# Gates laid out by feature, routing on the raw residual, and a finer last quad in each expert stage

## The reference, cut to what matters

```python
# first block, end
x = x + memory_cross_attention(...)              # o @ w_o
h = rmsnorm(x, ffn_norm)
g_logits = h @ wg_router + bg_router             # 4 groups
e_logits = h @ we_router + be_router             # 32 experts
# second block
gate_na, gate_mla = columns of (h @ w_in)        # 1024 wide each
merged = (sigmoid(gate_na)  * (y_na  @ w_proj_na)
          + sigmoid(gate_mla) * (y_mla @ w_proj_mla))
x = x + gate1 * (merged @ w_out)
h2 = rms_norm(x, g_norm2) * (1.0 + scale2) + shift2
# in both expert layers, for each expert e
a = silu(hg) * hu * gate[..., None];  out += a @ w_down[e]
shared = (silu(t @ w_sg) * (t @ w_su)) @ w_sd    # second block
```

## Time and profile before

| | us |
|---|---|
| median of 3 runs | 1127.06 (1125.6 to 1129.26) |
| profiled execution | 1125.87, span 1123.9 |
| PE busy | 988.9 (88%) |
| DVE busy | 461.2 (41%) |
| ACT busy | 206.0 (18%) |
| loads moved | 360.33 MB, mean 321 GB/s |
| mean granted clock of TensorE | 0.959 |

### The profile page before, as it was taken

How to read it: one execution, slowest core, us unless ns; L and a number is a source line. 1 busy time by engine, 2 the same in 40 slices (tenths; PEclk the granted TensorE clock), 3 DMA queues, 4 the chain that set the end, 5 groups by cost and what they waited for, 6 DMA issues and landing times.

```text
span 1123.9 us, 12966 instructions
## 1 busy us (share of the span) xinstructions
PE 988.9 (88%) x4504; PEld 477.8 (43%) x4504; DVE 461.2 (41%) x1089; ACT 206.0 (18%) x438; POOL 126.0 (11%) x167
## 2 busy tenths in 40 slices
PE   6999999887887677689999998998999998688777
PEld 4445543455332222144556544654544434233232
DVE  1796823345121111025754223677434335643234
ACT  2214301321111111021633403110211210000000
POOL 0000101000000000000000000005545543110000
PEclk9999999888998888899999999999999999889899
DMA  9744787978899999978984164079999997999997
GB/s 357 270 163 174 276 338 255 424 298 326 329 412 421 423 421 421 418 176 312 417 348 150 76 234 168 19 282 414 413 381 375 363 351 262 416 405 416 415 418 287
DMA packets 72272, 360.33 MB, mean 321 GB/s; under 512 B 19744, under 2 KB 21972, under 8 KB 45664
## 3 DMA queue, kind: packets, MB, share of 16 engines
q1 hardware_dynamic: 60816, 315.96, 70.9%
q0 software_dynamic: 11408, 43.74, 10.2%
HBM read 337.61 MB, written 30.31 MB: 327 GB/s over the span
## 4 chain that ended last, share of the span: by engine, by line
PE 71%; DMA 17%; DVE 5%; SPq 3%; ACT 2%; issue 2%; DVEq 0%; ACTq 0%
PE bank L998 31%; DMA wring<-in_w_pack 16%; PE bank L1265 9%; PE bank L1173 6%; PE bank L1123 5%; PE bank L1276 5%; PE bank L1206 4%; PE bank L1216 3%; PE bank L1009 2%; SPq L526 1%; PE bank L1363 1%; DMA wring<-in_w_ada 1%; PE bank L1063 1%; PE bank L1030 1%; PE bank L1037 1%
## 5 line engine op out<-in xcount | busy, mean ns | idle before, releaser
L998 PE MATMUL bank<-wring,hT 128*128 128x512 f32 (+3 forms) x608 | 248.5, 570 | 13.8 <-DVE hT L2637 8.5
L998 PEld LDWEIGHTS bank<-wring,hT 128*128 128x128 f32 x608 | 113.8, 200 | 139.4 <-issue 130.4
L1173 PE MATMUL bank<-wring,kT 128*32 128x512 f32 x944 | 119.8, 650 | 42.2 <-DMA wring<-in_w_pack 39.7
L1265 PE MATMUL bank<-wring,qT 128*128 128x512 f32 x256 | 114.6, 599 | 2.9 <-issue 2.9
L1173 PEld LDWEIGHTS bank<-wring,kT 128*32 128x32 f32 x944 | 30.9, 118 | 124.7 <-issue 71.6
L1216 PE MATMUL bank<-yT 128*128 128x512 f32 x128 | 65.1, 635 | 21.4 <-DVE yT L2508 5.7
L1206 PE MATMUL bank<-wring,yT 128*32 128x512 f32 x480 | 60.8, 626 | 23.2 <-DMA wring<-in_w_pack 14.3
L1265 PEld LDWEIGHTS bank<-wring,qT 128*128 128x128 f32 x256 | 48.3, 193 | 59.1 <-issue 59.1
L998 PE MATMUL bank<-wring,yT 128*128 128x512 f32 x160 | 70.5, 595 | 0.7 <-ACT yT L1622 0.7
L909 POOL DMA_INDIRECT PRT<-xn_parts_dram,part_now x64 | 65.6, 1025 | 28.4 <-issue 16.9
L1123 PEld LDWEIGHTS bank<-kT,x 128*128 128x128 f32 x512 | 62.8, 204 | 13.7 <-issue 11.6
(11 more groups left out here) (445 smaller groups left out, 1097.4 us busy)
## 6 DMA issues: line engine op xcount, KB each, us to landing
wring<-in_w_pack SPq DMA_DIRECT2D x132, 1024.0 KB, 15.3
wring<-in_w_pack SPq DMA_DIRECT2D x96, 512.0 KB, 14.8
wring<-in_w_pack SPq DMA_DIRECT2D x16, 2048.0 KB, 8.9
wring<-in_w_ada POOLq DMA_DIRECT2D x18, 1024.0 KB, 10.6
y_dram<-gateB SPq DMA_DIRECT2D x4, 4608.0 KB, 21.0
kT<-in_w_ada POOLq DMA_DIRECT2D x6, 1024.0 KB, 9.7
wring<-in_pack_z.0 SPq DMA_DIRECT2D x1, 2048.0 KB, 9.7
wring<-in_pack_z.2 SPq DMA_DIRECT2D x1, 2048.0 KB, 15.7
```

Source lines behind the costliest of these rows:

```text
L998: mm = nc.tensor.matmul(b[:, 0:n], lhs(k, t), w[:, k, c0:c0 + n], start=(k == 0), stop=(k == nk - 1))
L1173: mm = nc.tensor.matmul(bank[lane[j], 0, :], xqT[:, k, lane[j]], w[:, (k % 4) * 512:(k % 4 + 1) * 512], start=(k == 0), stop=(k == KD - 1))
L1265: mm = nc.tensor.matmul(bank[:, s, :], xT[:, s, k, :], item_gate_up(s)[:, k, :], start=(k == 0), stop=(k == KD - 1))
```

## The change

Five parts.

1. **Routing on the raw residual.** PE turns `x` itself as soon as `wo` is added; the gain goes in as before, and the factor per token is multiplied into the 36 logits on DVE, since it is one number per token. `tmp` is no longer written. The turns of t = 0 stand ahead of `wo.1.1`, and the logits of t = 0 between the two turns of t = 1.
2. **The list of experts later.** `quad_experts` and `experts_taken` move on DVE behind the hidden values of quad 1; on PE `experts_turned` moves behind its last down half, and the wait for the list to quad 2.
3. **Gates by feature.** `y.4` to `y.7`, `pna` and `pmla` are computed turned: the weights are held and 256 tokens stream. `merged0` and `merged1` are then the lower and the upper 512 features of all tokens, `wout2` reads them from `Z`, and `mgT` goes. The fixed experts' gate and up loads wait for the end of `wout2`, and the shared expert's weights are issued ahead of them.
4. **The last quad.** Down half 0 is loaded and computed in two pieces (its 256 hidden features in two halves of 128), four DMAs of 256 KB each, with one sum of half 1 between them and one behind.
5. **The shared down product sooner**, ahead of quad `duos + 3`.

`FIRST_BANK` moves by 4 in the second segment, as four bank uses go.

```diff
-    one += columns("wo", V)
-    for t in range(2):
-        one += [(f"xT3.{2 * t}", V), (f"xT3.{2 * t + 1}", V), (f"route1.{t}", V)]
+    one += [("wo.0.0", V), ("wo.1.0", V), ("wo.0.1", V), ("xT3.0", V), ("xT3.1", V), ("wo.1.1", V)]
+    one += [("xT3.2", V), ("route1.0", V), ("xT3.3", V), ("route1.1", V)]
...
+                if g == 1:
+                    piece(2, 0, 1024)
+                    piece(3, 1024, 1024)
+                else:
+                    piece(5, 1024, 1024)
+                    piece(4, 0, 512)
+                    piece(6, 512, 512)
...
-                sp.wait_ge(E("bank_filled"), group_at[f"mgT.{2 * s + 1}"][2])
+                sp.wait_ge(E("bank_filled"), group_at["wout2.1.1"][2])
                 load_item_gate_up(s, fixed_expert_of(s))
...
-                    if n == 1 and first:
-                        experts_turned(1)
+                    if second:
                         copied(pe, "items1")
...
                     else:
-                        down(0)
-                        combined(1)
-                    combined(0)
+                        down(0, (0,))
+                        pe.wait_ge(E(f"moe{n}_quad_half_copied"), i)
+                        combined_tile(0, 1)
+                        down(0, (1,))
+                        combined_tile(1, 1)
+                        combined(0)
...
+                    shared_down()
                     quad(duos + 3, False, ahead=3)
                     with pe.Fori(duos + 4, quads_n) as i:
                         quad(i, False)
-                    shared_down()
...
+            for n, t in ((0, 0), (1, 0), (0, 1)):
+                output_columns(n, t)
+                ada_steps(1)
+            residual_turned(0, 0)
+            residual_turned(0, 1)
+            output_columns(1, 1)
             pe.wait_ge(E("router_loaded"), 32)
+            residual_turned(1, 0)
+            b = opened("route1.0")
+            group_logits(b, 0, 0)
+            closed(group_logits(b, 0, 1))
+            residual_turned(1, 1)
+            b = opened("route1.1")
...
+            def turned_blocks(key, job, rows_, first_block, nk):
+                b = opened(key)
...
+                for j in range(2):
+                    c0 = P * (first_block + j)
+                    for k in range(nk):
+                        mm = nc.tensor.matmul(b[:, j * S:(j + 1) * S], w[:, k, c0:c0 + P], rows_[:, k, :], start=(k == 0), stop=(k == nk - 1))
...
+            pe.wait_ge(E("rows_ready"), ready_value("merged0"))
+            b = opened("wout2.0.0")
+            linear_steps(b, "wout2.0", merged_rows, 0, last=4)
+            b_next = opened("wout2.1.0", 1)
+            linear_steps(b_next, "wout2.1", merged_rows, 0, last=4)
+            pe.wait_ge(E("rows_ready"), ready_value("merged1"))
+            closed(linear_steps(b, "wout2.0", merged_rows, 0, first=4))
+            closed(linear_steps(b_next, "wout2.1", merged_rows, 0, first=4))
+            both_columns("wout2", ("wout2.0", "wout2.1"), merged_rows, 1, (0, 0))
...
                     hidden(1)
+                    quad_experts()
                     next_rows(1)
+                    experts_taken()
...
+                V.scalar_tensor_tensor(gl[:, t, :], b[:, 0:4], st[:, t:t + 1], rowv("router_group_b"), ALU.mult, ALU.add)
```

More of the change, by code:

```diff
@@ L194, in plan_groups @@
     for t in range(2):
-        two += [(f"mgT.{2 * t}", A), (f"mgT.{2 * t + 1}", A), (f"wout2.0.{t}", V), (f"wout2.1.{t}", V)]
+        two += [(f"wout2.0.{t}", V), (f"wout2.1.{t}", V)]
     for t in range(2):
@@ L1824, in y_columns, with gate_blocks @@
                 copy(f"y.{c}.{t}", Z[:, t, c0:c0 + w], func=func)
+            def gate_blocks(c, half):
+                c0 = (GN0, GM0)[c // 6] + 512 * half
+                copy(f"y.{c}.{half}", Z[:, c % 2, c0:c0 + 512], func=ACT.Sigmoid)
             for c in (0, 1, 3, 2):
```

151 lines of the change are left out of this document (92 added, 59 removed).

## The result

| | before | after |
|---|---|---|
| median, us | 1128.12 (1125.1 to 1134.29, 16 runs) | 1120.88 (1118.6 to 1127.11, 16 runs) |
| profiled execution, us | 1125.87 | 1119.93 |
| its span, us | 1123.9 | 1117.7 |
| ratio | | 0.9936, 95% interval 0.9922 to 0.9951 |

The change makes the kernel 0.64% faster, some 7 us. The sign was forecast, the size was not: 16.1 us and 1110.5 were, and 1120.88 lies above the forecast's range of 1107 to 1118. The profiled executions differ by 5.9 us.

A forecast was written before the change was run, and what follows sets the result against it. Full DMA stretches bound the kernel; their start and the work behind their last byte count. Terms 4.9 + 4.0 + 3.0 + 3.2 + 1.0 = 16.1 us off 1125.87 gave 1109.8, or 1110.9 from the median; forecast 1110.5, range 1107 to 1118.

The forecast's parts named there:

- parts 1 and 2, to quad 1's down: Routing and expert list ahead of the first stage: its full DMA stretch starts 8.9 us sooner, bounds 4.3 and 9.5.
- part 4, first stage's tail: Behind the first stage's last landing: split down half and earlier sums gain 3.0 us, after 0.3 for smaller loads.
- part 3, to the turn of the normed rows: Gates and wout2: sets of transposes and waits for copies go, gaining 3.2 us, bounds 2.7 and 3.8.
- part 5, and part 4 at the end: Second stage's end: moving the shared product gives 0, the split down half 1.0 us, bounds 0.3 and 1.3.
- the sentence on what is late next after part 2: Quad 2's down weights land at about 292.5, just when PE wants them; failure of this thin cover costs up to 2 us.
- part 2: List of experts ahead of quad 2's selection: selection starts 2.3 us sooner and keeps the upper clock; 4.0 us taken.
- the first stage keeps its start: Rival, chance 0.15: routing and list changes give 4 us instead of 8.9 at the first stage; time 1115.5.
- Its other ground: Same rival, first stage: the clock may fall earlier with so many small matmuls in a row; no separate size.
- low bounds of all terms together: Whole kernel: every term at its lowest gain gives 1117.6 us.
- part 1: First router: raw-residual routing brings the second logits forward, gaining 4.9 us; 2.0 if all at the lower clock.
- 0.3 us for the small pieces: First stage's last 2 MB: halving loads to 256 KB costs 0.3 us, bounds 0 and 1.
- weight loads: Case at the gates, chance 0.04: 256-column records, each with a weight load, take longer than half a 512-column one.

The follow-up runs named there:

- e10: Changed kernel with the last quad's old, unsplit down tail in the first expert stage alone; ratio 0.9928 to the kernel before.
- e1: Changed kernel with one 1 MB lane of the third quad's loads issued behind quad 2's down weights instead of ahead; ratio 0.9893 to the kernel before.
- e14: Changed kernel with 7 filler matmuls ahead of quad 2's down, where PE waits for its weights; ratio 0.9936 to the kernel before.
- e3: Changed kernel with 24 filler matmuls in PE's two gaps at the second router (16 and 8); ratio 0.9871 to the kernel before.
- e8: Kernel before with only the last quad's split down half, in both stages, shared product at its old place; ratio 0.9971 to the kernel before.
- e4: Kernel before with only the gates and projections by feature, with their wout2 and fixed loads; ratio 0.9987 to the kernel before.
- e6: Changed kernel with one lane behind quad 2's down weights, filler at the second router and the shared product at its old place; 1111.45 us, ratio 0.9842.
- e7: Kernel before with only the routing on the raw residual and the later list of experts; ratio 0.9936 to the kernel before.
- e2: Changed kernel with the shared product back at its old place, between the last quad but one and the last; ratio 0.9915 to the kernel before.
- e11: Changed kernel with 24 filler matmuls in the second stage's last quad, shared product at its new place; ratio 0.9938 to the kernel before.
- e9: Changed kernel with 24 filler matmuls ahead of quad 2's down; ratio 0.9956 to the kernel before.

## Why the prediction was half right

Step by step, in the profiled executions, gains in us:

| step | forecast | measured |
|---|---|---|
| parts 1 and 2, to quad 1's down | 8.9 | 9.4 |
| what of it reaches quad 2's second down | all | 4.1; 5.4 lost |
| part 4, first stage's tail | 3.0 | 2.9 from quad 2 to block 2, at most some 1 of it the new tail's (e10) |
| part 3, to the turn of the normed rows | 3.2 | 3.3 |
| second router | 0 | 4.1 lost |
| part 5, and part 4 at the end | 1.0 | 0 (3.5 and 3.4 us from the last packet to the add) |
| sum | 16.1 | 6.1 (6.14 at the adds) |

**The step that failed first** was the sentence on what is late next after part 2. It named the right weights, and it had them land at 292.5 with a failure worth "up to 2 us". They landed at 294.6, and 5.4 us were lost. The price was taken as the wait alone, and that too low: 2.4 of wait and 3.0 of lower clock behind it (e1, e14). The rival "the first stage keeps its start" is in the main this mechanism; its sum of 4 for parts 1 and 2 is what was measured, and it got 0.15. Its other ground, that many small matmuls in a row bring the clock down earlier, did not show: the clock fell at the end of the wait, between 294 and 296 us.

**The step that is missing** is the second router. The clock was weighed only at the places where the change removes a wait; I did not ask whether the stretches that the change does not touch keep theirs. The low bounds of all terms together gave 1117.6, and 1120.88 lies beyond it because no term held a loss of clock in an unchanged stretch. The row of the kernel before with 0.57 at 704 to 708 was there to see. e3 shows that the loss is the clock, e8 and e10 that it comes with part 4 of the first stage. So part 4 there gives 3.5 us to the kernel before and at most some 1 us beside parts 1 and 2, less 4.1 either way. Why a tail 210 us ahead decides it is not settled.

**Right in size:** part 1 (quad 1's selection 5.1 us sooner for 4.9), part 2 (4.3 us more up to quad 1's down for 4.0, the selection at 3.81 us, the upper level), part 3 (3.3 in the changed kernel and in e4, for 3.2), the tails on the kernel before (e8: 3.5 and 1.2), and 0.3 us for the small pieces. The gate records settle the case "weight loads", 0.04 in the forecast: that records of 256 columns, of which part 3 has 384 for 192 of 512, each with a weight load of its own, would take longer than half of one of 512. In the chain after, 32 of 256 columns take 6.91 us, 0.216 each, as in the earlier trace rows, so two take 0.432 where one of 512 took 0.429, and e4 shows a gain of 3.3. The eight loads of 256 KB at the end, issued by SyncE, cost an estimated 0.3 us together by e8 (386 GB/s for 411 over 2 MB).

```profile
547.78 6.91 PE bank L1563 x32
```

**Part 5** was priced at nothing because the last byte decides. With the shared product gone from the last quad the clock fell there in all eight profiles with the new place and no filler in that quad, and in two of the six with the old (e6, e7). The last byte comes no later, but PE is late for it by about 1 us, as much as part 4 gives at the end. The forecast 1.0 us there appears in e2 and e8 and not in the changed kernel.

With the three losses treated (e6) the gain is 17.8 us, interval 14.7 to 21.0, and the 16.1 of the sum lies in it. That does not confirm the sum term by term: the profile of e6, the slowest of its six executions, is 12.8 us ahead at the first add, and the filler gives 0.7 us at router 2 that the sum did not hold.

## What to carry to other kernels

When a change brings PE's work forward, list for the next two waits what is queued ahead of their loads and when that lands; a load that was just hidden can be the new wait, and its price was here the wait (2.4 us) and the lower clock behind it (3.0). When an idle gap of the DMA engines is used up, look at the order of the loads: 1 MB moved behind the down weights brought quad 2's second down from 302.1 to 296.1 (e1). Read PEclk also in the stretches that are not changed: where it falls briefly before, it may fall for long after (here 3.4 us, then 13.7). Of loads issued together, the one that is needed first goes first. Work that fills PE's gaps in a DMA-bound tail can be worth more there than elsewhere (about 1 us here by position, e2 and e11). And measure a part in the kernel that it will live in: the first stage's new tail was worth 3.5 us alone and at most 1 beside the other parts.

## What the runs showed of the hardware

- In otherwise equal stretches with gaps of 2.3 and 1.5 us in PE's work, the clock fell for 3.4 us, behind the second gap, in 4 of 4 profiles with the old first tail, and for 13.7 us, about at the end of the first, in 9 of 9 with the new and no filler. The length of the tail's own stretch at 0.50 does not divide the two groups; where the gap lies on the grid of 3.4134 us at which the clock changes does. What causes it was not found.
- With matmuls of 128 columns whose result nobody reads in the waits, the clock stood at 1.00 there: from 684 to 704 in e3, where the changed kernel has 0.50 from 687.8 to 701.5, and from 290 to 302 in e9 and e14, where it has 0.50 from 295.3 to 302.1. Such a matmul in fp32 is two records of 0.117 us, 0.234 together (5.62 over 48 in e9), where a turn is one. A filler longer than its gap delays what is behind it (3.2 us in e9, against e14).
- At the end of the second stage loads of 256 KB one behind the other ran at 386 GB/s and those of 512 KB at 411 (e8 and the kernel before). Slices of 1 MB loads in the first stage ran at 421 to 423.
